# A two-layer diffusion backbone on eight cores: second-layer conditioning loads later, token loads in chained pieces, and two of three FFN column groups done alone for the first tile

## The reference, cut to what matters

```python
m = jax.nn.silu(cond) @ w + b                     # adaln: 6 vectors of 1024 per layer
hp = rmsnorm(xp, norm_mix[i]) * (1.0 + mp[:, 1]) + mp[:, 0]
x, y = jnp.split(h @ w_in, 2, axis=-1)            # rglru_mixer: y = gelu(y); x = conv(x)
r, ig = sigmoid(gates of x)                       # block-diagonal, two directions
a = jnp.exp(-LRU_C * r * softplus(-lam)); bx = sqrt(1 - a*a) * (ig * x)
out = ((hf + hb) * y) @ w_out                     # hf, hb: forward and backward scans of a, bx
xp = xp + mp[:, 2] * op
hp = rmsnorm(xp, norm_ffn[i]) * (1.0 + mp[:, 4]) + mp[:, 3]
xp = xp + mp[:, 5] * ((jax.nn.silu(hp @ w_gate) * (hp @ w_up)) @ w_down)
```

## Time and profile before

| | |
|---|---|
| time, median of 3 | 1532.39 us (1531.67 to 1532.84) |
| time of the profiled execution | 1532.15 us |
| its span on the slowest core (core 6) | 1530.6 us |
| spans of cores 0 to 7 | 1517.4, 1529.7, 1529.6, 1517.4, 1529.7, 1516.5, 1530.6, 1517.2 us |
| PE busy | 1437.0 us (94%) |
| DVE, ACT, POOL busy | 906.6, 650.6, 225.7 us |
| DMA moved | 151.56 MB, mean 99 GB/s |

### The profile page before, as it was taken

How to read it: one execution, slowest core, us unless ns; L and a number is a source line. 1 busy time by engine, 2 the same in 40 slices (tenths; PEclk the granted TensorE clock), 3 DMA queues, 4 the chain that set the end, 5 groups by cost and what they waited for, 6 DMA issues and landing times.

```text
span 1530.6 us, 20044 instructions; the slowest of 8 cores (1516.5 to 1530.6 us)
## 1 busy us (share of the span) xinstructions
PE 1437.0 (94%) x6971; PEld 661.7 (43%) x6971; DVE 906.6 (59%) x1316; ACT 650.6 (43%) x866; POOL 225.7 (15%) x377
## 2 busy tenths in 40 slices
PE   4978996899999999999999999999999999999997
PEld 2433443444444445444444444444444444444444
DVE  1578695458687646528863364538856447744446
ACT  2597996548888234632013032632125013201023
POOL 6011021135231210011111100011110000101000
PEclk9999998999999999999999999999999999999999
DMA  9998368499435873554646754353332535985303
GB/s 176 171 191 129 49 110 193 57 156 146 74 60 86 168 137 55 84 83 70 110 69 97 117 101 72 56 83 56 55 63 47 86 55 93 198 142 87 65 1 110
DMA packets 50182, 151.56 MB, mean 99 GB/s; under 512 B 5410, under 2 KB 11042, under 8 KB 49572
## 3 DMA queue, kind: packets, MB, share of 16 engines
q0 software_dynamic: 45312, 133.32, 53.2%
q1 hardware_dynamic: 4772, 16.96, 3.4%
HBM read 270.94 MB, written 8.42 MB: 183 GB/s over the span
## 4 chain that ended last, share of the span: by engine, by line
PE 79%; DMA 9%; ACT 5%; issue 4%; DVE 3%; POOL 0%; DVEq 0%; ACTq 0%; POOLq 0%
PE pb L110 78%; DMA ringF<-modw 4%; DMA x_fm<-lru_in 2%; ACT h L105 1%; ACT reg L105 1%; ACT L105 1%; DMA x_fm<-xin 1%; DMA ringM<-lru_in 1%; DMA ringF<-ffn_d 1%; DVE x_fm L112 1%; DVE tmpn L112 1%; DMA tff<-lru_w_out 0%; ACT FS L105 0%; ACT x_fm L105 0%; DMA ringM<-lru_w_out 0%
## 5 line engine op out<-in xcount | busy, mean ns | idle before, releaser
L110 PE MATMUL pb<-h,ringF 128*128 128x512 bf16 x2624 | 585.7, 380 | 1.8 <-DVE FS L116 0.9
L110 PEld LDWEIGHTS pb<-h,ringF 128*128 128x128 bf16 x2624 | 255.3, 98 | 311.6 <-issue 9.3
L112 DVE SCALAR_TENSOR_TENSOR x_fm<-pb,modT,x_fm 128x512 f32<-128x512 f32 (+1 forms) x264 | 192.5, 733 | 196.6 <-PE pb L110 191.1
L110 PE MATMUL pb<-FS,ringF 128*128 128x512 bf16 x1312 | 296.6, 383 | 5.0 <-DVE x_fm L112 2.4
L105 ACT ACTIVATE tff<-pb 128x512 f32<-128x512 f32 x176 | 104.8, 596 | 385.7 <-PE pb L110 385.4
L112 DVE SCALAR_TENSOR_TENSOR tff<-tff,pb 128x512 f32<-128x512 f32 x176 | 120.2, 685 | 167.4 <-ACT tff L105 167.3
L110 PEld LDWEIGHTS pb<-FS,ringF 128*128 128x128 bf16 x1312 | 128.5, 99 | 161.8 <-issue 14.5
L116 DVE TENSOR_TENSOR FS<-tff,pb 128x512 bf16<-128x512 f32 x176 | 120.4, 685 | 68.8 <-PE pb L110 65.9
L105 ACT ACTIVATE h<-x_fm 128x1024 bf16<-128x1024 f32 (+2 forms) x86 | 84.2, 994 | 141.0 <-DVE x_fm L112 134.8
L105 ACT ACT_TABLE_LOAD x84 | 107.8, 1283 | 76.9 <-PE pb L110 69.3
L110 PE MATMUL pb<-h,ringM 128*128 128x512 bf16 x548 | 124.1, 380 | 4.3 <-DMA ringM<-lru_in 3.3
(11 more groups left out here) (152 smaller groups left out, 1252.3 us busy)
## 6 DMA issues: line engine op xcount, KB each, us to landing
ringF<-ffn_g POOLq DMA_DIRECT2D x45, 512.0 KB, 5.7
ringF<-ffn_u POOLq DMA_DIRECT2D x45, 512.0 KB, 6.9
ringF<-ffn_d POOLq DMA_DIRECT2D x36, 512.0 KB, 7.1
ringF<-modw POOLq DMA_DIRECT2D x34, 512.0 KB, 8.1
x_fm<-xin SPq DMA_DIRECT2D x4, 2048.0 KB, 14.3
yout<-x_fm SPq DMA_DIRECT2D x12, 512.0 KB, 8.3
ringM<-lru_in POOLq DMA_DIRECT2D x20, 256.0 KB, 5.6
ringM<-lru_w_out POOLq DMA_DIRECT2D x19, 256.0 KB, 5.7
```

Of the source, the lines that this page charges most:

```text
L110: "matmul": lambda e, a, k: e.matmul(*a, **k),
L112: "scalar_tensor_tensor": lambda e, a, k: e.scalar_tensor_tensor(*a, **k),
```

## The change

Six constants and three edits:

- `NSEG` 1 to 2: the first `ffn(0, 0)` call (stage 1) takes column groups 0 and 1 for tile 0 alone; the second (stage 4) takes groups 0 and 1 for tile 1 alone and group 2 for both. The weights of group 1 (8 gate/up loads and 4 down loads) are loaded twice.
- `MF` = 1: in the second call no mod piece is recorded in group 0; the eight are in group 1 and after. `SL1` = 3.0: the simulation assumes that a layer-1 mod piece lands 3 us later than before.
- `X4` = 3: `load_x4` replaces both loads of tiles 2 and 3. Four DMAs of 512 KB per tile on SP, each waiting until the one before has landed; tile 3 follows tile 2 in the same chain.
- `OSP1` 8 to 6: `out_proj` of tile 1 is recorded as 6 + 2 matmuls. `P1` 0.8 to 1.0: priority number of the LRU of tile 1.

```diff
-OSP, OSP1 = 6, 8
+OSP, OSP1 = 6, 6
-P1 = 0.8
+P1 = 1.0
-NP1, NSEG, NSET, NPR, NPB = 2, 1, 3, 1, 1
+NP1, NSEG, NSET, NPR, NPB = 2, 2, 3, 1, 1
+MF, SL1 = 1, 3.0
+X4 = 3
...
-        wv, wres = ring.load(desc, 1 << 20, prio=prio, slack=SLK if l == 0 and G > 0 else 0.0)
+        wv, wres = ring.load(desc, 1 << 20, prio=prio, slack=SL1 if l == 1 else SLK if G > 0 else 0.0)
...
+    def load_x4(tts, extra=()):
+        prev = list(extra)
+        for tt in tts:
+            for q in range(4):
+                t = P.dma("sp", "xs%d" % tt, lambda e: e.dma_start(out=x_fm[:, tt, 2 * q:2 * q + 2, :], in_=A["d_xin"][tt][:, 2 * q:2 * q + 2, :]),
+                          wr=[XR[(2 * q, tt)], XR[(2 * q + 1, tt)]], extra=prev, nbytes=1 << 19)
+                prev = [t]
...
-                if mods:
+                if mods and grp >= mfrom:
                     mod_piece(*mods.pop(0), prio=2)
...
+    if X4 & 1:
+        load_x4((2,), snapshot(KR[0:3] + [GK6]))
+        load_x4((3,), snapshot(LR[4].all() if M4 else KR[3:6] + [GK6]) + [P.tasks[-1]])
...
+    if X4 & 2:
+        load_x4((2, 3), xre)
...
-    ffn(0, 0, segs=..., mods=[(1, 0, kc) for kc in range(KC)])
+    ffn(0, 0, segs=..., mods=[(1, 0, kc) for kc in range(KC)], mfrom=MF)
```

More of the change, by code:

```diff
@@ L617, in emit_program, with ffn @@
     BM = Banks([4, 5, 6])
-    def ffn(l, hf, extra=(), mods=(), ep=1, after=None, segs=((0, (0, 1)), (1, (0, 1)), (2, (0, 1))), kept=None):
+    def ffn(l, hf, extra=(), mods=(), ep=1, after=None, segs=((0, (0, 1)), (1, (0, 1)), (2, (0, 1))), kept=None, mfrom=0):
         mods = list(mods)
@@ L1181, in emit_program @@
     P.prio = 1
-    load_x(2, extra=snapshot(KR[0:3] + [GK6]))
-    load_x(3, extra=snapshot(LR[4].all() if M4 else KR[3:6] + [GK6]))
+    if X4 & 1:
+        load_x4((2,), snapshot(KR[0:3] + [GK6]))
+        load_x4((3,), snapshot(LR[4].all() if M4 else KR[3:6] + [GK6]) + [P.tasks[-1]])
+    else:
+        load_x(2, extra=snapshot(KR[0:3] + [GK6]))
+        load_x(3, extra=snapshot(LR[4].all() if M4 else KR[3:6] + [GK6]))
     P.prio = PB
@@ L1194, in emit_program @@
     xre = snapshot(LR[5].all() + LR[6].all() + GWB)
[L1195 to L1201, removed]
+    if X4 & 2:
+        load_x4((2, 3), xre)
+    else:
+        for tt in (2, 3):
+            if XRP == 0:
+                load_x(tt, extra=xre)
+                continue
+            for q in range(4):
+                P.dma("pool", "xq%d" % (4 * (tt - 2) + q), lambda e: e.dma_start(out=x_fm[:, tt, 2 * q:2 * q + 2, :], in_=A["d_xin"][tt][:, 2 * q:2 * q + 2, :]),
+                      wr=[XR[(2 * q, tt)], XR[(2 * q + 1, tt)]], extra=xre, nbytes=1 << 19, prio=XRP)
     out_proj(0, "d_lru_w_out", (2, 3), BM, ringM)
@@ L1205, in emit_program @@
     cm_setup(BM)
-    ffn(0, 0, segs=((0, (1,)), (1, (0, 1)), (2, (0, 1))) if NSEG == 1 else ((0, (1,)), (1, (1,)), (2, (0, 1))), mods=[(1, 0, kc) for kc in range(KC)])
+    ffn(0, 0, segs=((0, (1,)), (1, (0, 1)), (2, (0, 1))) if NSEG == 1 else ((0, (1,)), (1, (1,)), (2, (0, 1))), mods=[(1, 0, kc) for kc in range(KC)], mfrom=MF)
     ffn(0, 1, mods=[(1, G, kc) for G in (1, 2) for kc in range(KC)])
```

## The result

The changed kernel took 1557.14 us (median of 4 runs, 1551.53 to 1566.7) beside 1532.62 for the kernel before on the same chip: ratio 1.0161, 95% interval 1.0115 to 1.0207. On a second chip the ratio was 1.011 (1.0073 to 1.0147). The forecast was 1518 us, faster; the kernel became 17 to 25 us slower.

What follows compares the result with a forecast made beforehand. It took PE as the bound, its empty time lying mostly before 300 us, 14.7 us of it one mod wait. The sum -20.0 - 2.0 + 7 + 1 = -14 us against 1532.15 gave 1518 us, range 1508 to 1530.

Steps and rivals of the forecast that it cites:

- the wait and its dummies go: Before tile 1's output projection: 192 group 1 matmuls replace PE's 14.73 us mod wait and dummies, -20.0 us.
- LRU B ... it can be done, with little air: First FFN matmul of tile 1 to projection of tiles 2 and 3: ACT and DVE run 13.6 us faster, +1 us.
- The bound of +9: Upper bound of the LRU B term, whose bounds were 0 and +9 and whose taken value was +1.
- rival B: LRU B is bound by ACT; PE waits for `reg` and `x_fm`, +9 instead of +1, 1527 us; chance 0.13.
- a piece costs 4.4 us and eight cost 35: First token load of tiles 2 and 3: chained 512 KB SP pieces take 4.4 us each, 230 to 265 us.
- The trace agrees, and on it rests: Queues alternate packet by packet, so a chained SP piece in flight still takes two thirds of a DMA engine.
- Rival C: Slow chain, 8.3 us a piece; tile 3's column sum holds PE, +22; 1537 us (1532 to 1542); chance 0.11.
- the column sums on PE: Sums of tiles 2 and 3, at about 255 and 276 us: no wait at 4.4 us a piece.
- the +7: DMA contention in the new group 1 stretch: 2.3 to 2.5 loads short at 3.1 us, bounds 0 and +14.
- the norm's 13 us stay: Norm of tile 1, 283.64 to 296.94: chain through ACT and DVE, covered by no FFN work in either order.
- second token load 0: Second load of tiles 2 and 3: fifth piece, landing after 22 us, is hidden at 4.4 us a piece; 0.
- other mod waits, -2: Nine more PE waits for mod pieces, 6.3 us in all: part goes, -2.0 us, bounds 0 and -6.3.

Runs made afterwards that it cites:

- d_m: The kernel before with only the later conditioning pieces (MF = 1, SL1 = 3.0), OSP1 = 6 and P1 = 1.0; ratio 1.0056 to the kernel before.
- a_swap: The changed kernel in its own recorded order, only the 32 conv-diagonal TENSOR_SCALARs moved from POOL to DVE; ratio 1.0048 to the kernel before.
- b_swap: The kernel before in its own recorded order, only its conv-diagonal TENSOR_SCALARs moved from POOL to DVE; ratio 1.0008 to the kernel before.
- u_x4: The changed kernel without chained token loads (X4 = 0, tiles 2 and 3 loaded as before); ratio 1.0016 to the kernel before.
- d_nseg: The kernel before with only NSEG = 2; ratio 1.0062 to the kernel before.
- d_x4: The kernel before with only the chained token loads (X4 = 3 and load_x4); ratio 1.0076 to the kernel before.
- a_thin: The changed kernel in its own order, each conv-diagonal TENSOR_SCALAR on POOL writing 8 of its 128 columns; ratio 1.0054 to the kernel before.
- a_q: The changed kernel with the same 512 KB quarters on SP, a tile's quarters not waiting for each other; ratio 1.0055 to the kernel before.

## Why the prediction was wrong

- **Right: the wait and its dummies go.** 14.73 us became nothing, `modw` waits fell from 21.0 to 2.6 us. What the prediction did not see is whose wait it was: `d_m` shows that without group 1 in its place it returns as 12.29 us for `lru_w_out`. Group 1 (NSEG = 2) is what covers it.
- **Failed, the largest: "LRU B ... it can be done, with little air", +1 us.** Measured +16.6. The step argued from the busy shares of ACT and DVE that 13.6 us less PE work would let the stage end 13.6 us sooner. The stage took 3 us longer instead. What holds it is a loop through several engines that none of them fills: PE's convolution frees the diagonals, POOL builds them beside DVE's scans, and only then issues the `lru_in` load that PE's next matmuls need. By `a_swap`, 6.5 us of the 16.6 are that block in the changed kernel's own order; a new order with it gone takes 12. Of the other 10 some 6 are the gate/up matmuls at the end, behind DVE's last scans, and 1.8 are waits for `ffn_d`, both read from traces and not tested; the rest is open. The kernel before has the same block and shows nothing of it (`b_swap`), so it could not be read from its waits. The bound of +9 was from ACT's load, and rival B named ACT and DVE, whose shares over 90 us fell. What could be read beforehand was POOL's slow blocks themselves, and the planner's 0.4 us for each diagonal in the code.
- **Failed: "a piece costs 4.4 us and eight cost 35".** 8.9 us in the median and 63 us for the eight. The 4.4 rested on two thirds of each DMA engine for a piece in flight, read from 2 MB transfers with many packets waiting. With chained 512 KB pieces SP's queue got 27.7% of the time. "The trace agrees, and on it rests" was one step too far: the rows showed turns between two full queues, not between a full one and one piece. Rival C had 8.3 us a piece and +22; the price was 16. C had the direction and the piece nearly right, but its 1537 us (1532 to 1542) holds nothing for LRU B either.
- **Failed: where late tokens hurt.** I watched the column sums on PE. They did wait (2.25 and 1.87 us), but more came through ACT, whose squares stand ahead of the FFN's activations (2.17 and 3.69 us), and from the lower clock behind each wait. The waits for `ffn` loads that the +7 was made of were 1.0 us, not 4 to 10. So A-B cost 16 us in place of 7: right in kind only without the chains, where PE does wait for `ffn` loads (3.8 us per core in `u_x4`, whose A-B of 9.2 less 19.4 is -10, near the -13 of the sum; 8.4 in `d_nseg`).
- **Half right: the norm's 13 us stay, and nothing else between projection and FFN.** The norm took 14.6 us (324.85 to 339.43, core 3), 1.3 more. But B-C grew by 2 to 6 us in every kernel with NSEG = 2, chained or not, and by 4 in `d_x4`. On core 3 the projection has a 3.15 us wait for `lru_w_out` and 2.8 us of slow matmuls behind it; in the kernel before (core 6) the wait was 1.5 us. The cause was not isolated.
- **Failed in size: second token load 0.** D-E grew by 3 to 5 us with SP's quarters (`d_x4` 4.9 alone).
- **About right: other mod waits, -2.** E-F fell by 2.3 us on the first chip. The later pieces may be worth more: on each of four other chips the kernels that have them lost 4 to 8 us less in E-F than those that do not (25.1 and 26.6 against 30.4 and 31.0 on one). The prediction had no term for that.

Together: -20 +16 +5 +17 +3 -2, and 5 us more on the slowest core, against -20 +7 +0 +1 +0 -2.

## What to carry to other kernels

Before counting on the work that you move out of a stage, compare the stage's duration in two orders with different amounts of filler: a loop through several engines that the filler hid may hold it. Where the durations agree, ask in each what PE waits for; it need not be the same. Read the timelines of the engines with small busy shares inside one turn of the loop. A wait names the load that came last, not the transfer that made it late; only work put in its place, or that transfer moved, ends it. Cutting a transfer into pieces that wait for one another gave its bandwidth to the other queue here (64.4% of the engines' time before, 27.7% after), and each engine that waits for a piece holds up all that stands behind it in its list.

## What the runs showed of the hardware

- A TENSOR_SCALAR of 128x128 on POOL took 0.59 us with DVE quiet and, in the changed kernel, 1.3 to 2.7 beside DVE's scans and two-input products; with 8 columns still up to 3.78 (`a_thin`). The same on DVE took 0.31 us.
- On core 3 of the changed kernel, from 230 us on, ten of eleven waits of PE of 2.2 to 3.7 us were followed by slow matmuls, 1.5 to 2.9 us lost behind each; waits up to 1.9 us lost at most 0.2. It is not a rule: in `a_swap` (core 5) a wait of 2.56 us lost nothing.
- Two DMA queues took turns one packet for one (576 to 609) with four 512 KB transfers outstanding on SP (`a_q`), and 353 to 755 with one (the changed kernel).
